# Gated delta rule: inverse kept on exchanged halves, both directions scanned in one step, mask in the exponent, fillers placed anew

## The reference, cut to what matters

```
gcum = cumsum(g);  decay = exp(where(i >= j, gcum_i - gcum_j, -inf))
k_beta = k * beta
a_kk = where(i > j, (k_beta k^T) * decay, 0)
t_inv = inverse(eye + a_kk)                      # 64 x 64, for each chunk and head
u = t_inv (v * beta);  w = t_inv (k_beta * exp(gcum))
qk = (q k^T) * decay;  q_dec = q * exp(gcum);  k_dec = k * exp(gcum_last - gcum)
for each chunk:
    v_new = u - w state
    o = q_dec state + qk v_new
    state = state * exp(gcum_last) + k_dec^T v_new
bidir: o = forward(q, k, v, beta_0, g_0) + flip(forward(flip(q), ..., g_1))
o = rmsnorm(o, dn_out_norm_g) * silu(z);   y_dn = o @ w_o_dn
```

## Time and profile before

| | |
|---|---|
| median of 3 runs | 3067.24 us (3065.84 to 3069.03) |
| profiled execution | 3080.82 us |
| its span on the core | 3078.6 us |
| TensorE matmuls busy | 2835.6 us, 92% of the span |
| VectorE busy | 2186.0 us, 71% |
| ScalarE busy | 1566.6 us, 51% |
| GpSimd busy | 116.1 us, 4% |
| mean granted TensorE clock | 0.961 |

### The profile page before, as it was taken

One profiled execution on the slowest core, in us unless ns is written; L12 is line 12 of the kernel. 1 busy time (PEld: TensorE's weight loads), 2 busy tenths in 40 slices (PEclk: granted clock), 3 DMA queues, 4 the chain that ended last, 5 costly groups with the idle time before them and its releaser, 6 DMA issues.

```text
span 3078.6 us, 47399 instructions
## 1 busy us (share of the span) xinstructions
PE 2835.6 (92%) x20496; PEld 2436.7 (79%) x20496; DVE 2186.0 (71%) x2198; ACT 1566.6 (51%) x1478; POOL 116.1 (4%) x134
## 2 busy tenths in 40 slices
PE   7988999998989999999999999798889989888998
PEld 7867799886768787787878777687878868777896
DVE  4556655556759888897988879677566857756685
ACT  3344443354447676676767667455234435523442
POOL 0000000000000000000000000001300000030000
PEclk9899999999989999999999999898999999899999
DMA  5343554444349999898999999642034445302442
GB/s 184 102 134 130 175 191 167 157 156 139 116 175 339 333 344 328 327 352 315 344 329 348 327 322 356 221 139 96 17 104 149 147 152 163 108 30 77 152 165 96
DMA packets 360216, 616.20 MB, mean 200 GB/s; under 512 B 13760, under 2 KB 117056, under 8 KB 359984
## 3 DMA queue, kind: packets, MB, share of 16 engines
q1 hardware_dynamic: 354784, 597.50, 55.6%
q0 software_dynamic: 5200, 15.34, 2.1%
HBM read 611.75 MB, written 1.05 MB: 199 GB/s over the span
## 4 chain that ended last, share of the span: by engine, by line
PE 76%; DVE 13%; ACT 5%; issue 4%; DMA 1%; POOL 0%; ACTq 0%; DVEq 0%; SPq 0%; POOLq 0%
PE ps L658 22%; PE ps L660 21%; PE ps L659 21%; PE ps L1042 4%; DVE wlo L1504 3%; ACT whi L1147 3%; DVE co L2301 2%; PE ps L890 1%; PE ps L921 1%; PE ps L911 1%; DVE co L2299 1%; PE ps L751 1%; DVE W L2226 1%; PE ps L1115 0%; PE ps L736 0%
## 5 line engine op out<-in xcount | busy, mean ns | idle before, releaser
L1504 DVE TENSOR_TENSOR wlo<-raw,whi 128x2048 fp32r<-128x2048 f32 (+2 forms) x588 | 1302.3, 2221 | 464.2 <-ACT whi L1147 459.9
L1147 ACT ACTIVATE whi<-raw 128x2048 fp32r<-128x2048 f32 (+2 forms) x588 | 1090.0, 1858 | 472.2 <-PE ps L660 459.9
L658 PE MATMUL ps<-whi,xTh 128*128 128x512 f32 (+5 forms) x1488 | 601.4, 404 | 30.4 <-issue 16.8
L659 PE MATMUL ps<-wlo,xTh 128*128 128x512 f32 (+5 forms) x1488 | 589.8, 396 | 0.0
L660 PE MATMUL ps<-whi,xTl 128*128 128x512 f32 (+5 forms) x1488 | 588.9, 396 | 0.0
L658 PE MATMUL ps<-xTh,whi 128*128 128x256 f32 x1504 | 431.4, 287 | 23.8 <-DVE xTl L1511 11.6
L660 PE MATMUL ps<-xTh,wlo 128*128 128x256 f32 x1504 | 429.3, 285 | 0.0
L659 PE MATMUL ps<-xTl,whi 128*128 128x256 f32 x1504 | 427.2, 284 | 0.0
L658 PEld LDWEIGHTS ps<-whi,xTh 128*128 128x128 f32 x1488 | 293.2, 197 | 96.9 <-issue 21.5
L660 PEld LDWEIGHTS ps<-whi,xTl 128*128 128x128 f32 x1488 | 291.9, 196 | 64.4
L659 PEld LDWEIGHTS ps<-wlo,xTh 128*128 128x128 f32 x1488 | 292.9, 197 | 59.2
(11 more groups left out here) (519 smaller groups left out, 3616.4 us busy)
## 6 DMA issues: line engine op xcount, KB each, us to landing
raw<-in_expert_w_dram SPq DMA_DIRECT2D x336, 1024.0 KB, 5.7
raw<-in_w_in_dram SPq DMA_DIRECT2D x76, 1024.0 KB, 5.1
raw<-in_w_up_dram SPq DMA_DIRECT2D x44, 1024.0 KB, 5.2
raw<-in_dense_w_dram SPq DMA_DIRECT2D x32, 1024.0 KB, 5.2
raw<-in_w_down_dram SPq DMA_DIRECT2D x20, 1024.0 KB, 5.6
raw<-in_w_out_dram SPq DMA_DIRECT2D x16, 1024.0 KB, 5.0
raw<-in_w_branch_diff_dram SPq DMA_DIRECT2D x8, 1024.0 KB, 5.0
raw<-in_w_ple_gate_dram SPq DMA_DIRECT2D x8, 1024.0 KB, 4.9
```

Of the source, the lines that this page charges most:

```text
L658: self.e.matmul(out, ah, bh, start=start, stop=False)
L659: self.e.matmul(out, ah, bl, start=False, stop=False)
L1147: self.e.activation(self.m.hi[u % NHL][:, 0:n], self.m.raw[u % NRAW][:, 0:n], ACT.Copy) \
L1504: self.e.tensor_tensor(self.m.lo[u % NHL][:, 0:n], self.m.raw[u % NRAW][:, 0:n], self.m.hi[u % NHL][:, 0:n].bitcast(F32), ALU.subtract) \
```

## The change

In words, for each of the two layers:

- `blocks` takes several products at once, each with the half of the rows (i) and of the columns (j) on which it lies. The first T of a direction is formed in memory that is free at that time (`first_inverse`): GpSimd masks A into it (step `M0`), VectorE subtracts it from the unit matrix. `t0` makes T on exchanged halves and TT on its own, two products on four quarters. `lu` makes its two products on four quarters, and VectorE subtracts them in two operations, first the transpose (W1), which `lq` waits for, then T (W0), which `lu` waits for.
- The scan takes chunk n of both directions in one step. The states of both lie in one tile. q_dec times state and qk v_new are accumulated in PSUM; in step 0 ScalarE copies the result into `odn`, in step 1 VectorE adds it. For this `odn` and `zs` keep the chunks in another order: the z epilogue is cut into three operations on ScalarE and VectorE, and odT's copies too.
- The triangular mask goes into the exponent: the clip at 0 becomes a maximum with a mask of 0 and 1e30 (two more mask tables), and GpSimd's multiplication of Q falls away. GpSimd multiplies zs with the gain ng instead of VectorE multiplying odn in `dend`, and makes kd (at k = 3 and 4).
- R is formed at k = 5 ahead of VectorE's part of `lu` (step `dr`); `du` takes both directions, all of u first.
- The fillers: one between the `qkT` of tile 0 and those of tile 1, one ahead of `du` of step 0, one between `dend` and `odT`, one behind `odT`.

```diff
 def delta(self, l, fill):                      # Plan
-        o += fill[0:1]
-        for t in range(2):
-            o += [("qkT", l, t, 0), ("qkT", l, t, 1)]
-        o += fill[1:2]
+        o += [("qkT", l, 0, 0), ("qkT", l, 0, 1)] + fill[0:1] + [("qkT", l, 1, 0), ("qkT", l, 1, 1)]
+        o += [("M0", l, 0, d) for d in range(2)]
         for step in range(2):
             K = [(l, step, d) for d in range(2)]
             o += [("t0",) + k for k in K]
             for k in range(1, 6):
+                scan = step == 1 and k < 3
                 o += [("lq", k) + c for c in K]
-                if step == 1 and k < 3:
-                    o += [("s1", l, 0, d, k - 1) for d in range(2)]
+                if scan:
+                    o += [("s1", l, 0, k - 1)]
+                if k in (3, 4):
+                    o += [("kd",) + K[k - 3]]
+                if k == 5:
+                    o += [("dr",) + c for c in K]
                 o += [("lu", k) + c for c in K]
-                if step == 1 and k < 3:
-                    o += [("s2", l, 0, d, k - 1) for d in range(2)]
-            o += [("du",) + k for k in K]
+                if scan:
+                    o += [("s2", l, 0, k - 1)]
+            o += fill[1:2] if step == 0 else []
+            o += [("du", l, step)]
+            if step == 0:
+                o += [("M0", l, 1, d) for d in range(2)]
         for n in range(2):
-            o += [("s1", l, 1, d, n) for d in range(2)] + [("s2", l, 1, d, n) for d in range(2)]
-        o += [("dend", l)] + fill[2:]
+            o += [("s1", l, 1, n), ("s2", l, 1, n)]
+        o += [("dend", l), fill[2], ("odT", l)] + fill[3:]
...
-    def blocks(self, ps, o, left, right):
+    def blocks(self, ps, *products):
         for h in range(8):
             for c in range(2):
-                r = slice(64 * c, 64 * c + 64)
-                ins = self.e.matmul(ps[r, o + h * 64:o + h * 64 + 64], left[r, h * 64:h * 64 + 64], right(c, h),
-                                    start=True, stop=True)
+                for o, left, right, i, j in products:
+                    ri, rj = slice(64 * (c ^ i), 64 * (c ^ i) + 64), slice(64 * (c ^ j), 64 * (c ^ j) + 64)
+                    ins = self.e.matmul(ps[rj, o + h * 64:o + h * 64 + 64], left(ri, h), right(ri, h), start=True, stop=True)
...
         if what == "t0":
             e.wait_ge(*self.at("T0", *K))
-            ps = self.fill(key, ("TT",) + K)
-            ins = self.blocks(ps, 0, T, lambda c, h: m.mk[64 * c:64 * c + 64, 3, :])
+            ps = self.fill(key, ("T",) + K)
+            ins = self.blocks(ps, (512, U, eye, 0, 0), (0, eye, U, 0, 1))
         elif what == "lq":
-            ins = self.blocks(ps, 0, m.E[d], of(TT))
+            ins = self.blocks(ps, (0, of(m.E[d]), TT, 0, 1))
...
-            ins = self.blocks(ps, 512, T, of(Q))
             if k < 5:
-                ins = self.blocks(ps, 0, Q, of(T))
+                ins = self.blocks(ps, (512, T, Q, 1, 0), (0, Q, T, 1, 1))
+            else:
+                ins = self.blocks(ps, (512, T, Q, 1, 0))
...
+            for h in range(8):
+                for d in range(2):
+                    ins = e.matmul(ps[rows[d], w(h):w(h) + 64], m.dwT[d][half(h), h // 2, rows[d]], S[half(h), d, h // 2, :],
+                                   start=True, stop=True)
...
-            e.tensor_scalar(m.E[d], m.E[d], 0.0, None, ALU.max).then_inc(*self.up("d_delta", ("e1",) + a))
+            e.tensor_tensor(heads(m.E[d]), heads(m.E[d]), mask(16 + d), ALU.max).then_inc(*self.up("d_delta", ("e1",) + a))
...
         elif what == "lu":
             k, ps = a[0], self.psum("lu", *a)
-            w, o = (m.W[d][:, :, :].rearrange("p a b -> p (a b)"), 0) if k < 5 else (m.W[d][:, 1, :], 512)
             e.wait_ge(*self.at("full", "lu", *a))
-            e.tensor_tensor(w, w, ps[:, o:1024], ALU.subtract).then_inc(*self.up("d_delta", ("W",) + a))
+            for j in (1, 0) if k < 5 else (1,):
+                w = m.W[d][:, j, :]
+                e.tensor_tensor(w, w, ps[:, 512 * j:512 * j + 512], ALU.subtract).then_inc(*self.up("d_delta", (f"W{j}",) + a))
```

More of the change, by code:

```diff
@@ L483, in up, with first_inverse @@
         return sem, by
+    def first_inverse(self, K):
+        _, step, d = K
+        return self.m.A[d][d] if step else self.m.kd[d]
     def psum(self, *key):
@@ L1105, in delta_scan @@
+            ins.then_inc(*self.up("mm_delta", ("full", "s1") + N))
+            ps = self.fill(("o",) + N, ("od",) + N)
+            self.open.add(self.p.slot[("o",) + N])
+            for h in range(8):
+                for d in range(2):
+                    ins = e.matmul(ps[rows[d], w(h):w(h) + 64], m.qdT[d][half(h), h // 2, rows[d]], S[half(h), d, h // 2, :],
+                                   start=h < 2, stop=False)
+            ins.then_inc(*self.up("mm_delta", ("full", "sq") + N))
             return
@@ L1117, in delta_scan @@
-        ins.then_inc(*self.up("mm_delta", ("full", "o") + K4))
-        if not first:
-            self.on_state(("sq",) + K4, ("oq",) + K4, m.qdT[d], S, r)
-    def on_state(self, key, free, left, S, r):
-        ps = self.fill(key, free)
-        for h in range(8):
-            half, w = slice(64 * (h % 2), 64 * (h % 2) + 64), h % 2 * 512 + h // 2 * 64
-            ins = self.e.matmul(ps[r, w:w + 64], left[half, h // 2, r], S[half, h // 2, :], start=True, stop=True)
-        ins.then_inc(*self.up("mm_delta", ("full",) + key))
+            for d in range(2):
+                e.wait_ge(*self.at("kd", l, step, d))
@@ new lines, in delta_scan @@
+        if first:
+            e.wait_ge(*self.at("u", l, step, 0))
+            e.wait_ge(*self.at("u", l, step, 1))
+        else:
+            e.wait_ge(*self.at("vn", *N))
+        ps = self.fill(("s2",) + N, ("S",) + N)
+        for h in range(8):
+            for d in range(2):
+                o = 512 * (n ^ d) + h // 2 * 64
+                ins = e.matmul(ps[half(h), o:o + 64], m.kd[d][rows[d], h * 64:h * 64 + 64], m.u[n][rows[d], h * 64:h * 64 + 64],
+                               start=True, stop=True)
@@ new lines, in delta_scan @@
+        ins.then_inc(*self.up("mm_delta", ("full", "s2") + N))
+        if first:
+            ps = self.fill(("o",) + N, ("od",) + N)
+        else:
+            ps = self.psum("o", *N)
+            e.wait_ge(*self.at("full", "sq", *N))
+        for h in range(8):
+            for d in range(2):
+                ins = e.matmul(ps[rows[d], w(h):w(h) + 64], m.qkT[step ^ d][d][rows[d], h * 64:h * 64 + 64],
+                               m.u[n][rows[d], h * 64:h * 64 + 64], start=first, stop=first or h > 5)
@@ new lines, in delta_scan @@
+            e.wait_ge(*self.at("full", "s1", *N))
+            part = bands(self.psum("s1", *N))[:, :, 0:256].rearrange("p a (r n) -> p a r n", r=4)
+            e.tensor_tensor(halves(m.u[n][:, :]), halves(m.u[n][:, :]), part, ALU.subtract) \
+                .then_inc(*self.up("d_delta", ("vn",) + N))
+            e.wait_ge(*self.at("full", "o", *before))
+            for d in range(2):
+                g = m.gt[:, n ^ d, step ^ d, 4 * d:4 * d + 4].unsqueeze(2).broadcast_to([128, 4, 64])
+                ins = e.tensor_tensor(new[:, d], old[:, d], g, ALU.mult)
```

274 lines of the change are left out of this document (160 added, 114 removed).

## The result

The changed kernel took 3042.7 us (median of 6 runs, 3034.7 to 3051.5) against 3070.7 for the kernel before in the same runs: a ratio of 0.991, 95% interval 0.9887 to 0.9933. It is faster, by 28 us, or 14 a layer; I had said 36 a layer and 2995 us, and 3042.7 lies above the range too. The profiled execution took 3049.9 us, its span 3048.1.

The account below looks back on a forecast made before the run. It took TensorE's array to bound the inverse loop. Per layer 21.2 + 32.4 + 39.7 + 13.5 = 106.8 us instead of 142.7, so 35.9 less, 72 for both: 3067 - 72 = 2995 us, range 2979 to 3026.

Parts of the forecast that it names:

- front, to the first t0: From the start of the k/q transposes to the first inverse: 21.2 us a layer instead of 32.5.
- t0 to the end of the filler: Step 0's inverse, 22.6 us a layer, then a filler of 5.7.
- use, step 1, scan: Step 0's du, 4.1 us a layer, then step 1 and the scan, 39.7 instead of 55.5.
- tail: After the scan, to the first product with w_o_dn: 13.5 us a layer instead of 14.85, odT between the last fillers.
- parts 2 and 3: Step 0's inverse, filler and use, 32.4 us a layer; step 1 and the scan, 39.7 us.
- the chain settles at 4.1 us a round: Inverse loop: VectorE's four operations make rounds of 4.1 us, against 6.20 before, with lu on four quarters at 1.16.
- The split z epilogue: Front: two more operations each on ScalarE and VectorE delay the transposes by 2.2 us a layer.
- 0 to 2 us per layer, taken as 0: Front: the longer pause ahead of the transposes may lower the clock; no cost was put into the sum.
- Rival B: Inverse loop: row halves sharing a PSUM bank hamper each other, rounds 5.65 us, 15.6 a layer, 3026 us; chance 0.12.
- rival C: Handovers and ports cost more, the loop is bound by latency: 8 us a layer, 3011 us; chance 0.22.
- D: First t0 to scan's end: clock granted at 1.2 GHz, 23 us a layer slower, 3113 us; chance 0.03.
- No wait on Q: Sign that the forecast is right: TensorE waits no more than 1 us on Q or the first inverse.

Follow-up runs that it names:

- the bare products: Separate kernel without the network, only products with ready operands; 3072 instructions took about 41 us on four quarters, 45.0 us on two.
- the shift of the pauses: Changed kernel with 32 small products (128 instructions) more at the head of the delta rule; 3040.5 us in its one run.

## Why the prediction was wrong

The sign was right; the size was 2.6 times too large. By parts, from the kernel before's start of the transposes (z's epilogue + 2.43 us in both kernels), us per layer:

| part | predicted | measured | miss |
|---|---|---|---|
| front, to the first t0 | 21.2 | 23.7 | +2.5 |
| t0 to the end of the filler | 28.3 | 35.8 | +7.5 |
| use, step 1, scan | 43.8 | 56.3 | +12.5 |
| tail | 13.5 | 13.1 | -0.4 |

- **The step that failed** is the rate of the loop in parts 2 and 3: "the chain settles at 4.1 us a round, against 4.06 of TensorE". I took the array as TensorE's only limit and carried 64 product records in 1.16 us, seen in one Gram product at a time, over some 5800 instructions. Rounds took 5.55 us in the mean. The missing limit, one block of 256 instructions in 3.85 us, accounts for both stretches within 0.5 us, and the bare products, the shift of the pauses and the packets that land ahead of each pause show it. How long the loop would take with more supply no run shows. It could not be read from a wait in the kernel before: at 28 ns for a product and its weight load, 14 ns an instruction, its groups ran at just about the supply's rate, so its rows looked like a bound by the array. What could have been seen was the clue: 19 instruction packets in 85 us, as many as a loop at that pace uses up.
- **Front.** The split z epilogue was priced at 2.2 us and cost 2.4 in waiting. The clock behind the longer pause, "0 to 2 us per layer, taken as 0", was another 2.3, above even its own range: 5.13 us instead of 2.80 to the first Gram product. That is the whole miss of the front; its other terms stood in sum.
- **Rival B** named rounds of 5.65, close to the 5.55 that came, by a mechanism that is refuted: lu groups took 1.2 us and banks shared by row halves cost nothing in the bare products. A hit on the number would have been no evidence. Of rival C's signs one came, a GpSimd mask of 3.33 us; lq never waited on W. D's clock near 0.5 in the loop did not come: it was 1.00 there.
- **What held.** No wait on Q, none on the right-hand sides (0.9 us had been left for them), the first inverse waited 1.0 us at a time; the transposes of the output between the fillers left no pause behind the second.
- **What the gain consists of.** The kernel before with the new places gains 0.33% of its time, all the rest of the change with the old places 0.23%, together 0.9%. The medians' excess over the sum is 11 us, with an interval of 9 each way; the stretches of both layers give 7.9, 8.1 and 29.9 us, an excess of 14, so the parts need each other. About 2 us of it a layer lie ahead of the first t0, the rest behind it; that it lies in pauses that each part leaves to the other, and in the clock behind them, I only argue. The scan in one step and the mask in the exponent were not priced alone, and stay open.

## What to carry to other kernels

Count TensorE's instructions as a resource beside its busy time: in the long runs of small products here, their number times 13.5 to 15 ns was a floor (one block of 256 in 3.45 to 3.85 us), and packing more quarters didn't lower it; wider products did more within it (64x128 took the time of 64x64 in the bare products). When a loop is near that floor, spend the effort on where the long products stand, and on the pauses ahead of them: a wait of 3.0 us was followed by half the clock, one of 0.65 us was not. Price a change's parts in both combinations: the places and the rest of the change were worth 10 and 7 us alone and 28 together. And look at both layers of a trace before you read a difference of 2 us from one.

## What the runs showed of the hardware

- TensorE was given 256 instructions in 3.45 us at best (13.5 ns each), 3.85 us in this network's loop. The store ahead hid one block's delay: in the bare products the first pause came after 382 instructions.
- The pauses followed the packets of 16384 bytes on the instruction queue: each ended 1.2 to 1.6 us after one had landed, and the next packet started 1.0 to 1.5 us after a pause of such a run had ended.
- This rate was the same with the granted clock at 1.00 (40.7 and 41.5 us for 3072 instructions) and at 0.55 (41.7, bf16).
- A 64x64 fp32 product record on two diagonal quarters was issued every 29 ns, on four every 15 ns; whether two row halves wrote one PSUM bank or not made no difference (25.1 us of work for 1536 either way).
- A wait of 3.0 us ahead of 128x128 transposes was followed by 5.2 us at 1.2 GHz; one of 0.65 us, by none.
